# Gated heads of a decoder layer on TensorE: the 16 meta tokens moved to partitions 64 to 79, and the order of the four state products

## The reference

```python
def gla(q, k, v, g_out, gate_lr, w2, b2, norm_g):
    ...
    P = GLA_CHUNK - N_META                 # chunks of 64; the first holds only the 16 meta tokens
    ...
    q_in = qc * jnp.exp(b)
    k_in = kc * jnp.exp(-b)
    A = jnp.einsum('bhnid,bhnjd->bhnij', q_in, k_in)
    A = jnp.where(tril, A, 0.0)
    o_intra = jnp.einsum('bhnij,bhnjv->bhniv', A, vc)
    chunk_kv = jnp.einsum('bhncd,bhncv->bhndv', kc * jnp.exp(b_last - b), vc)
    decay = jnp.exp(b_last[:, :, :, 0, :])
    def step(S, inp):
        dec, kv = inp
        return dec[..., None] * S + kv, S
    ...
    o_inter = jnp.einsum('bhncd,bhndv->bhncv', q_in, S_prev)
```

## Time and profile before

| | |
|---|---|
| median of 3 runs | 1235.96 us |
| profiled execution | 1235.84 us |
| its span, first to last instruction | 1234.1 us |
| TensorE (PE) busy | 1212.3 us, 98% |
| weight loads (PEld) busy | 1149.1 us |
| DVE, ACT, POOL busy | 673.5, 602.7, 487.7 us |
| granted TensorE clock, mean | 0.995 of 2.4 GHz |
| DMA | 212.31 MB, 172 GB/s |

### The profile page before, as it was taken

How to read it: one execution, slowest core, us unless ns; L and a number is a source line. 1 busy time by engine, 2 the same in 40 slices (tenths; PEclk the granted TensorE clock), 3 DMA queues, 4 the chain that set the end, 5 groups by cost and what they waited for, 6 DMA issues and landing times.

```text
span 1234.1 us, 23737 instructions
## 1 busy us (share of the span) xinstructions
PE 1212.3 (98%) x8954; PEld 1149.1 (93%) x8954; DVE 673.5 (55%) x956; ACT 602.7 (49%) x908; POOL 487.7 (40%) x224
## 2 busy tenths in 40 slices
PE   9899999999999999999999999999999999999997
PEld 9799999999989998999999999999999988888885
DVE  6774646554565348666666666666666643232224
ACT  7344444455655437544444444444444544444444
POOL 1233333333344433344444444444444444434443
PEclk9899999999999999999999999999999999999999
DMA  9545454544445563565665655665655565655551
GB/s 330 166 145 158 138 170 137 163 122 128 142 149 176 181 196 121 162 187 173 187 183 174 187 182 174 187 183 174 187 182 175 187 201 181 195 189 186 194 163 69
DMA packets 175695, 212.31 MB, mean 172 GB/s; under 512 B 6688, under 2 KB 162720, under 8 KB 175520
## 3 DMA queue, kind: packets, MB, share of 16 engines
q1 hardware_dynamic: 175216, 210.32, 55.1%
q10 hardware_dynamic: 432, 1.34, 0.3%
HBM read 209.53 MB, written 2.10 MB: 171 GB/s over the span
## 4 chain that ended last, share of the span: by engine, by line
PE 91%; DVE 5%; ACT 1%; SPq 1%; DMA 1%; issue 1%; DVEq 0%; ACTq 0%
PE psum L410 66%; PE psum L1754 19%; PE psum L1400 1%; DVE a_lo L1233 1%; DMA raw<-in_w_in 1%; DVE w_lo L394 1%; DVE a_lo L940 1%; PE psum L1565 1%; ACT w_hi L390 1%; PE psum L1455 1%; SPq L384 1%; PE psum L1782 0%; PE psum L1481 0%; PE psum L1583 0%; DVE xT L1249 0%
## 5 line engine op out<-in xcount | busy, mean ns | idle before, releaser
L394 POOL TENSOR_TENSOR w_lo<-raw,w_hi 128x1024 fp32r<-128x1024 f32 x192 | 473.0, 2463 | 723.6 <-ACT w_hi L390 723.6
L410 PE MATMUL psum<-a_hi,w_hi 128*128 128x258 f32 (+1 forms) x2360 | 676.1, 286 | 3.5 <-DVE w_lo L394 1.4
L410 PE MATMUL psum<-a_lo,w_hi 128*128 128x258 f32 (+1 forms) x2360 | 674.4, 286 | 0.0
L410 PE MATMUL psum<-a_hi,w_lo 128*128 128x258 f32 (+1 forms) x2360 | 670.7, 284 | 0.0
L390 ACT ACTIVATE w_hi<-raw 128x1024 fp32r<-128x1024 f32 x391 | 411.6, 1059 | 480.7 <-PE psum L410 347.6
L394 DVE TENSOR_TENSOR w_lo<-raw,w_hi 128x1024 fp32r<-128x1024 f32 x200 | 264.0, 1320 | 417.9 <-ACT w_hi L390 416.8
L410 PEld LDWEIGHTS psum<-a_hi,w_hi 128*128 128x128 f32 x2360 | 448.9, 190 | 9.9 <-issue 5.5
L410 PEld LDWEIGHTS psum<-a_lo,w_hi 128*128 128x128 f32 x2360 | 449.1, 190 | 0.0
L410 PEld LDWEIGHTS psum<-a_hi,w_lo 128*128 128x128 f32 x2360 | 446.8, 189 | 0.1
L1291 DVE SCALAR_TENSOR_TENSOR proj<-proj,par 128x256 f32<-128x256 f32 x88 | 112.9, 1283 | 40.6 <-ACT proj L806 40.6
L1754 PE MATMUL psum<-w_lo,a_hi 128*128 128x512 f32 x336 | 131.9, 393 | 0.0
(11 more groups left out here) (234 smaller groups left out, 629.5 us busy)
## 6 DMA issues: line engine op xcount, KB each, us to landing
raw<-in_w_up SPq DMA_DIRECT2D x176, 512.0 KB, 3.6
raw<-in_w_in SPq DMA_DIRECT2D x95, 512.0 KB, 4.0
raw<-in_w_down SPq DMA_DIRECT2D x88, 512.0 KB, 4.0
raw<-in_w_out SPq DMA_DIRECT2D x32, 512.0 KB, 3.7
xT<-in_features SPq DMA_DIRECT2D x3, 544.0 KB, 7.4
temp<-in_post_ffn_g ACTq DMA_DIRECT2D x1, 1024.0 KB, 7.9
out<-proj SPq DMA_DIRECT2D x2, 512.0 KB, 2.7
out<-proj SPq DMA_DIRECT2D x4, 256.0 KB, 2.8
```

Source lines behind the costliest of these rows:

```text
L394: eng.tensor_tensor(w_lo[:, j % SPLIT, :], raw[:, j, :], w_hi[:, j % SPLIT, :], ALU.subtract)\
L410: mm = pe.matmul(psum[:, bank + m, 0:t1 - t0], w[:, j % SPLIT, cols], a[:, k, t0:t1], start=(k == 0 and step == 0), stop=(k == KT - 1 and ...
```

## The change

The meta tokens' keys and values are put on partitions 64 to 79 (`META`) where they were on 0 to 15. To get them there a transpose takes 80 columns as its source: the 64 columns ahead of the tile (the end of the tile before it in `proj`) and the 16 meta columns, and the last 16 of its 80 results are used (`gla_transposes`). For the first tile of the values those 64 columns hold nothing yet, so POOL clears them at the start, and TensorE waits for that once. The meta product of A takes 16 stationary columns instead of 128 and writes to partitions 64 to 79. The state products come in the order chunk 1 (rows 0 to 63), chunk 0 (64 to 79), chunk 3 (0 to 63), chunk 2 (64 to 127). ACT's copies and DVE's operations on the meta rows follow to the new partitions.

```diff
+        META = slice(64, 64 + n_meta)
...
             masked(c_mask[:], 0.0, [[-1, n_meta]], Q0, 1, ALU.is_ge, MASKED).then_inc(consts_made, 1)
+            pool.memset(tile(T_VG - 1)[:, n_tok - META.start:n_tok], 0.0).then_inc(consts_made, 1)
...
-                            copy(vg_nat[0:n_meta, 0, v * P:(v + 1) * P], src[0:n_meta, 0, :]).then_inc(free(step, v), 1)
+                            copy(vg_nat[META, 0, v * P:(v + 1) * P], src[META, 0, :]).then_inc(free(step, v), 1)
...
-                        copy(k_nat[0:n_meta, 0, :], src[0:n_meta, 0, :]).then_inc(free(step), 1)
+                        copy(k_nat[META, 0, :], src[META, 0, :]).then_inc(free(step), 1)
...
-                        dve.tensor_scalar(a_T[0:n_meta, 2 * P:2 * P + NM],
-                                          psum[0:n_meta, bank_of(step, 1), 2 * P:2 * P + NM], BIGGEST, -BIGGEST,
+                        dve.tensor_scalar(a_T[META, 2 * P:2 * P + NM],
+                                          psum[META, bank_of(step, 1), 2 * P:2 * P + NM], BIGGEST, -BIGGEST,
...
-                        dve.tensor_tensor(a_T[0:n_meta, 2 * P:2 * P + NM], a_T[0:n_meta, 2 * P:2 * P + NM],
-                                          block_T[0:n_meta, Q0:n_meta], ALU.mult).then_inc(free(step, 1), 1)
+                        dve.tensor_tensor(a_T[META, 2 * P:2 * P + NM], a_T[META, 2 * P:2 * P + NM],
+                                          block_T[META, 64 + Q0:64 + n_meta], ALU.mult).then_inc(free(step, 1), 1)
...
+            def gla_transposes(bank, t):
+
+                return transposes(bank, [(0, proj[:, t * n_tok - META.start:t * n_tok + n_meta])] +
+                                  [(n * P, tile(t)[:, TOKENS[n][0]:TOKENS[n][1]]) for n in (1, 2)])
...
+                if hd == 0:
+                    pe.wait_ge(consts_made, 8)
                 for v in range(2):
                     await_free(pe, step, v)
-                    transposes(bank_of(step, v), [(n * P, tile(T_VG + 2 * hd + v)[:, a:a + P])
-                                                  for n, (a, _) in enumerate(TOKENS)]).then_inc(full(step, v), 1)
+                    gla_transposes(bank_of(step, v), T_VG + 2 * hd + v).then_inc(full(step, v), 1)
...
-                transposes(bank_of(step), [(n * P, k_dec[:, a:a + P]) for n, (a, _) in enumerate(TOKENS)])\
-                    .then_inc(full(step), 1)
+                gla_transposes(bank_of(step), T_V + 6).then_inc(full(step), 1)
...
-                pe.matmul(psum[:, bank, 2 * P:2 * P + NM], k_in[:, 0:P], q_in[:, Q0:n_meta], start=True, stop=True)
+                pe.matmul(psum[META, bank, 2 * P:2 * P + NM], k_in[:, 0:n_meta], q_in[:, Q0:n_meta], start=True, stop=True)
...
-                for c, rows, t in ((0, slice(0, n_meta), 0), (1, slice(0, 64), 1), (2, slice(64, P), 1),
-                                   (3, slice(0, 64), 2)):
+                for c, rows, t in ((1, slice(0, 64), 1), (0, META, 0), (3, slice(0, 64), 2), (2, slice(64, P), 1)):
...
-                    mm = pe.matmul(psum[:, bank_of(step, 1), v * NM:(v + 1) * NM], vg_nat[0:n_meta, 0, v * P:(v + 1) * P],
-                                   a_T[0:n_meta, 2 * P:2 * P + NM], start=True, stop=True)
+                    mm = pe.matmul(psum[:, bank_of(step, 1), v * NM:(v + 1) * NM], vg_nat[META, 0, v * P:(v + 1) * P],
+                                   a_T[META, 2 * P:2 * P + NM], start=True, stop=True)
```

## The result

The changed kernel takes 1238.45 us (median of 22 executions, 1236.91 to 1238.84), the kernel before 1236.13 us beside it: ratio 1.0018, 95% interval [1.0012, 1.0024]. It is 2.3 us slower. The forecast was 1237.2 with a range up to 1238.2; the measured time lies 0.25 us above the range, on the side that was forecast, with nearly twice the loss. Of the 0.25, 0.17 is the base: the forecast was added to a median of three, 1235.96, where the kernel before now has 1236.13.

The account below looks back on a forecast made before the run. TensorE was taken to bound the gated heads, so each nanosecond there counts. State products +0.76, head 0's entry +0.09 and the meta product of A +0.40 gave +1.25 on 1235.96: 1237.2 us, range 1233.4 to 1238.2.

Parts of the forecast that it names:

- (e): ACT's copies, DVE's operations and a POOL memset beside TensorE in the gated heads: sizes kept, no cost, 0.
- State steps: State products of four gated heads: between -0.62 and +0.19 us a head; upper end taken, +0.76 in all.
- overlap rivals: 16-row block runs beside the 64-row one in state steps: full overlap 1234.0 us (chance 0.17), half overlap 1234.7 (0.18).
- Entry of head 0: Head 0's first state product, now 64 rows, follows 16-row products: a change of height, +0.09 us once.
- Key step: Meta product of A with 16 stationary columns: its load comes later, +0.10 us a head, +0.40 in all.
- 80-column transposes: First of each three transposes takes 80 columns instead of 128: neither gain nor loss, 0.
- slower rival: The 12 80-column transposes count as another shape and stop the array: +0.36 us each, 1241.5 us, chance 0.06.
- Behind the heads: Stages after the gated heads: the heads' rounding moves with the last chunk; no cost priced there.
- nothing arrives: Drift of some 1 us is taken up in waits where the stage ends: 1236.0 us, chance 0.07.
- (c): Meta product of A narrowed to 16 columns, in each head: +0.10 us taken, ends 0 and +0.21.

Follow-up runs that it names:

- order alone: The kernel before with only the new order of the state products, meta rows staying on partitions 0 to 15: 1237.29 us, ratio 1.0006.
- height alone: The changed kernel with its meta state product 64 rows high (partitions 64 to 127, rows 80 to 127 zero): 1235.19 us, ratio 0.9992 to the kernel before.
- 128-column A: The changed kernel with 128 instead of 16 stationary columns in the meta product of A: 1238.30 us, ratio 1.0015 to the kernel before.

## Why the prediction was wrong

The sign was right and so was the array; the sum was 1.25 and the loss is 2.3, and what was missing did not come from the terms that had been priced. Two things were put at nothing: what runs beside, part (e), which cost 0.37, and all that lies behind the heads, where the other 0.65 of the median is put by the profiles. With the first alone the time would be 1236.13 + 1.67 = 1237.8, inside the range; the second took it out. The cause of the first is shown, that of the second is open.

- **State steps**, upper end taken, +0.19 a head: measured +0.20 (1.88 instead of 1.68), in all four heads. The choice between the ends, made by the nearest row, was right: order alone gives 1.88, equal height gives 1.06. Both overlap rivals are out: the 16-row block beside a 64-row one on the other half overlaps with nothing. The rule of the Trainium skill ("TensorEngine Tiling (Array Packing)", Key Properties) that a change of mode drains the array and a change of tile does not is what the runs show, now with disjoint rows too. The Trainium skill ("TensorE: Matmul & The Clock Gate", Part 3, The mechanism) says that a load overlaps with matmuls in flight only when the row group differs; a differing group is not enough here: in the changed kernel the groups differ and the load waits 0.30 behind the last pass.
- **Entry of head 0**, +0.09: the 64-row load stands 0.20 behind the last 16-row load (246.27 to 246.47), as priced.
- **Key step**, +0.10: the step is 0.10 to 0.11 longer in heads 0, 2 and 3, with the 16-column load 0.20 behind the last transposing pass and the next load 0.13 behind it. Right.
- **80-column transposes**, 0: they start 0.11 apart. The slower rival never came up.
- **What runs beside**, (e), is the step that failed in the heads. It said that ACT's and DVE's operations "keep their sizes and only move to partitions 64-79", and so cost nothing. Their durations hardly move (249 to 267 ns on ACT), but the distance to the operation behind them grows: 0.5 us for a head's value copies, and on DVE the clamp behind the 2-column one starts 0.17 instead of 0.07 us later. And the cover for that was named wrongly, as a side step two chunks on. ACT's queue holds the weight splits, DVE splits behind ACT, and the PSUM bank of the next key step is freed behind that: in head 1 the slack was smaller than 0.5 us, and TensorE paid 0.37. In the other heads it was larger. With it, 1.25 becomes 0.80 + 0.09 + 0.40 + 0.37 = 1.66, and the stretch shows 1.67.
- **Behind the heads**, put at nothing: the prediction had everything behind the stretch move with it at its old length, named "a clock below 1.00 in the stretch" as something outside it, and looked for it in the heads only. The stretch leaves 0.65 us of the median, and the place where a loss shows is the passage to the MLP: there two of two profiled executions of the changed kernel lost 0.84 and 1.11 us at clock 0.50 to 0.55 and that of before none. That is the other step that failed. The w_out stage behind the heads is TensorE-bound and hands the delay on exactly (100.76 both times); the passage behind it has idle time and passes of one column. Why some executions drop there is open. It is not mere lateness: the kernel that is 1.7 us early (height alone) has an unexplained 0.77 like those that are 1.4 to 2.1 late, and those shifted by 0.4, 0.9 and -2.5 have little or none. Nor is it the place in time alone: the first one-column pass of the passage stands at 459.10 and 459.12 us in the two executions of the changed kernel, at 459.04 in that of the new order alone and at 459.14 in that of the 128-column A, and these two kept clock 1.00.
- The rival "nothing arrives" had it backwards: the stages behind took up nothing of the delay, and the passage added to it.

The range was too narrow on its upper side for the same reason: it held the unknown of (c) and the scatter, but no entry for a wait on another engine and none for the clock at a place that the change doesn't touch.

## What to carry to other kernels

In all these runs two small products ran side by side on TensorE only where their stationary blocks had the same height and lay on different rows. To pair a short one with a taller one, pad it to the other's height with zeros: here 48 rows of zeros turned 1.88 us a head into 1.06. An operation that only changes its start partition still has to be priced on its engine, by the distance to the next start, and followed through everything queued behind it; keeping all partitions in one operation was cheaper than addressing 16. The clock can drop at a stage that the change doesn't touch, in some executions and not in others, so compare stages between the same instructions, not only totals.

## What the runs showed of the hardware

- ACT: a copy that starts on partition 64 between copies from partition 0. Four copies take 1.35 us to the next operation instead of 0.84; an 80-partition copy from partition 0 instead of a 16-partition one from 64 brings it back to 0.85. It is the start that counts, not the number of partitions. On DVE the clamp on 2 columns at partition 64 adds 0.10 us to the one behind it (0.17 instead of 0.07).
- TensorE: 16 rows on partitions 64 to 79 run beside 16 rows on 0 to 15 (loads interleaved from 245.68 to 245.87 us), but not beside 64 rows on 0 to 63.
- Two pairs of 64-row products on alternating halves follow each other with no stop: eight loads within 0.73 us.
